# Four reciprocal square roots move from GpSimd to ScalarE, and three weight splits change place in a two-block transformer kernel

## The chip, the cores and the metric
The kernel runs on one core of one Trainium2 chip. The metric is the device time of one execution in microseconds (us), from the first to the last work of the program. Five engines work side by side and meet only at semaphores: TensorE (PE: matmuls and transposes), VectorE (DVE), ScalarE (ACT), GpSimd (POOL) and SyncE (SP), which here issues the loads from HBM.

## The reference
Two transformer blocks of two layers each run one after the other on 256 tokens of 1024 features, all in float32. Cut to what matters here:

```python
for i in range(2):                                   # first block
    xn = rmsnorm(h, norm_mix[i])
    h = h + hybrid_mixer(xn, w_in[i], ...)           # differential, forgetting and retention heads
    xn = rmsnorm(h, norm_ffn[i])
    h = h + (swiglu(...) if i == 0 else moe_swiglu(...))      # dense, then 8 experts, top 2
    gate = sigmoid(rmsnorm(h, ple_norm[i]) @ ple_gate[i])
    h = h + gate * (p[i] @ ple_proj[i])
# in hybrid_mixer, for the four differential heads of 128 columns:
    o_a = o[:, :, 0] - lam * o[:, :, 1]
    o_a = rmsnorm(o_a, subln_g) * (1 - lam_init)     # root 1: 8 roots a token row (2 tiles x 4 heads)

for l in range(2):                                   # second block
    proj = rms_norm(x, norm_g[l]) @ w_in[l]          # q_a, k_a, v_a, q_h, f_h, i_h, q_m, z
    kv_m = rms_norm(mem, mem_norm_g[l]) @ w_mem_kv[l]
    km = rms_norm(k_m, mem_k_norm[l])
    qm = rms_norm(q_m, mem_q_norm[l])                # root 2: again 8 a row
    y = concat([o_a, o_h, o_m]) * silu(z)
    x = x + y @ w_out[l]
```

## The kernel before, in words
Tokens lie in two tiles of 128 partitions. Every weight is streamed once from HBM in pieces of 1 MB (128 partitions x 2048 numbers). To get float32 accuracy from TensorE, ACT copies a piece to `high` in a rounded format (`split` in the ACT program, L1364), DVE subtracts it from the raw piece to get `low` (L1847), and PE does three matmuls for each product: high by high, high by low and low by high (`exact`, L700 to L702). So each piece goes SP load, ACT high, DVE low, then 24 (or 48 narrower) matmuls on PE. Activations are split in the same manner: PE turns rows, ACT writes the high half of the turned rows (L1380), DVE the low half (L1869).

There is no scheduler. Each engine has its program written out by hand, and the place of a split in it is set by calls: `splits(done)` makes all pieces up to three beyond `done` that have not been made, `split_next()` makes the next one. Only three `high`/`low` buffers exist, so ACT's `high` of a piece waits until PE has used the piece three before it (`pieces_used`). An engine works strictly in its own order; what stands behind an instruction that waits, waits too.

A reciprocal square root is asked for in two ways. `rstd_ask` writes mean square plus epsilon into `stat` on DVE, ACT answers with Sqrt (`serve_sqrt`, L1388), DVE takes the reciprocal (`rstd_answer`, L1900). ACT keeps one set of function tables; between Exp (the softmax, L1472) and Sqrt stands a table load. The second way, `root_ask`, hands the same `stat` to POOL, which raises it to the power -0.5 (L1835), and DVE goes on at `root_answer` without a reciprocal. It serves four places: in `attention1` of each layer (steps i == 9 and 10), for the differential heads, and in `attention2` (steps 2 and 3), for the memory queries `qm`. `attention1` and `attention2` are software pipelines over 12 heads: at step i, PE makes scores of head i, turns the weights of head i-1 and multiplies values for head i-2, and between these does the projections of later weights. In `attention1` the projections end with i == 9; at i == 10 ACT takes `v` and `sg` out of banks 6 and 7, PE then writes the turned retention queries and keys there (L875), and ACT goes on to Exp of head 10.

The expert layer is followed by a branch on an overflow flag (ACT L1718, DVE L2526, PE too). In its usual arm stands `embedding_in(1)`, which makes two splits with `split_next()`: one at its start and one at its end. Behind the branch follow `splits`, the memory rows' norm (`mem_sums`, `mem_norm`) and `embedding_out` on PE. Below, pg0 and pg1 are the two halves of the first gate weight of layer 1, pg2 the next piece, km0, km1, vm0, vm1 and qa0 the pieces of the memory keys, memory values and first queries of the second block, in the order of the stream.

## Time and profile before
| | |
|---|---|
| time, median of 3 runs | 2024.94 us (2024.91 to 2027.08) |
| the profiled execution's own time | 2024.91 us |
| its span, first to last instruction | 2023.1 us |
| PE, DVE, ACT, POOL busy | 97%, 76%, 61%, 0% |
| read from HBM | 501.73 MB, 249 GB/s over the span |

PE is busy for nearly the whole span, so what counts is time in which PE stands still. A timeline row reads: start, duration, engine, line, operation, and in brackets the idle time before it with what ended it. Matmuls overlap: the distance between starts, not the duration, is the pace (about 0.23 us for 512 columns at the full clock).

### The profile page before, as it was taken

The numbers are of one execution on the slowest core, as the hardware profiler recorded it, in microseconds if no ns is written. First come the engines' busy times: TensorE is split into PE (matmuls) and PEld (weight loads), VectorE is DVE, ScalarE is ACT, GpSimd is POOL, SyncE is SP. The second block draws the span as 40 slices with busy tenths as digits, with TensorE's granted clock in tenths as the row PEclk, the third lists the DMA queues.
The fourth block names the chain that finished last, engine by engine and source line by source line (L and its number), as shares of the span: only waits on it lengthen the run. The fifth ranks groups of instructions, "written<-read, shape, count | busy, mean of one in ns | idle before, by whom it ended". The sixth has DMA issues, their size and how long they took to land.

```text
span 2023.1 us, 27402 instructions
## 1 busy us (share of the span) xinstructions
PE 1960.2 (97%) x10513; PEld 1670.3 (83%) x10513; DVE 1541.1 (76%) x1509; ACT 1232.5 (61%) x1332; POOL 6.8 (0%) x8
## 2 busy tenths in 40 slices
PE   8999999999899999999999999999998998999998
PEld 7879998887788888888888888888887887888887
DVE  5565555656788988889888898888887855876576
ACT  4555445554677777777777777777777544354442
POOL 0000000000000000000000000000000000000000
PEclk9999999999999999999999999999999999999999
DMA  8607554522799999999999999999976541345311
GB/s 262 223 30 268 188 187 147 173 99 80 266 374 351 351 375 330 373 342 359 373 330 374 340 359 375 330 374 336 363 290 220 187 161 69 125 155 199 126 63 42
DMA packets 243316, 504.08 MB, mean 249 GB/s; under 512 B 12184, under 2 KB 59032, under 8 KB 243224
## 3 DMA queue, kind: packets, MB, share of 16 engines
q1 hardware_dynamic: 242936, 502.71, 69.7%
q8 instruction: 63, 1.03, 0.2%
q14 instruction: 29, 0.24, 0.0%
q10 hardware_dynamic: 288, 0.11, 0.0%
HBM read 501.73 MB, written 1.05 MB: 249 GB/s over the span
## 4 chain that ended last, share of the span: by engine, by line
PE 83%; DVE 10%; ACT 4%; issue 2%; DMA 0%; DVEq 0%; ACTq 0%
PE bank L700 25%; PE bank L702 25%; PE bank L701 25%; DVE low L1847 4%; ACT high L1364 2%; PE bank L1171 1%; PE bank L1119 1%; PE bank L671 1%; PE bank L824 1%; ACT high L1566 1%; PE bank L1271 1%; DVE negmax L2029 1%; PE bank L793 1%; PE bank L815 1%; DVE y_lo L2482 1%
## 5 line engine op out<-in xcount | busy, mean ns | idle before, releaser
L2433 DVE TENSOR_TENSOR low<-raw,high 128x2048 fp32r<-128x2048 f32 x336 | 768.4, 2291 | 103.8 <-ACT high L1566 102.4
L1566 ACT ACTIVATE high<-raw 128x2048 fp32r<-128x2048 f32 x336 | 644.8, 1920 | 245.5 <-PE bank L702 244.7
L1847 DVE TENSOR_TENSOR low<-raw,high 128x2048 fp32r<-128x2048 f32 (+1 forms) x138 | 310.4, 2260 | 177.8 <-ACT high L1364 177.4
L1364 ACT ACTIVATE high<-raw 128x2048 fp32r<-128x2048 f32 (+1 forms) x138 | 260.7, 1894 | 170.2 <-PE bank L702 155.0
L700 PE MATMUL bank<-high,xg_hi 128*128 128x512 f32 x896 | 353.6, 395 | 0.8 <-DVE xg_lo L2416 0.8
L702 PE MATMUL bank<-high,xg_lo 128*128 128x512 f32 x896 | 349.5, 390 | 0.0
L701 PE MATMUL bank<-low,xg_hi 128*128 128x512 f32 x896 | 348.8, 389 | 0.0
L700 PE MATMUL bank<-high,xT_hi 128*128 128x512 f32 (+1 forms) x576 | 226.8, 394 | 5.7 <-issue 2.1
L702 PE MATMUL bank<-high,xT_lo 128*128 128x512 f32 (+1 forms) x576 | 221.5, 385 | 0.0
L701 PE MATMUL bank<-low,xT_hi 128*128 128x512 f32 (+1 forms) x576 | 221.0, 384 | 0.0
L700 PE MATMUL bank<-high,hT_hi 128*128 128x512 f32 x536 | 210.1, 392 | 0.0
L701 PE MATMUL bank<-low,hT_hi 128*128 128x512 f32 x536 | 208.7, 389 | 0.0
L702 PE MATMUL bank<-high,hT_lo 128*128 128x512 f32 x536 | 208.7, 389 | 0.0
L700 PE MATMUL bank<-xT_hi,high 128*128 128x256 f32 x672 | 193.2, 288 | 5.4 <-ACT v L1512 2.3
L702 PEld LDWEIGHTS bank<-high,xg_lo 128*128 128x128 f32 x896 | 168.1, 188 | 35.8
L700 PEld LDWEIGHTS bank<-high,xg_hi 128*128 128x128 f32 x896 | 168.3, 188 | 34.9 <-issue 1.1
L701 PEld LDWEIGHTS bank<-low,xg_hi 128*128 128x128 f32 x896 | 168.4, 188 | 33.7
L701 PE MATMUL bank<-xT_lo,high 128*128 128x256 f32 x672 | 191.3, 285 | 0.0
L702 PE MATMUL bank<-xT_hi,low 128*128 128x256 f32 x672 | 191.3, 285 | 0.0
L700 PEld LDWEIGHTS bank<-xT_hi,high 128*128 128x128 f32 x672 | 130.3, 194 | 7.3 <-ACT v L1512 2.7
L700 PEld LDWEIGHTS bank<-high,xT_hi 128*128 128x128 f32 x576 | 108.3, 188 | 27.8 <-issue 3.0
L701 PEld LDWEIGHTS bank<-xT_lo,high 128*128 128x128 f32 x672 | 130.3, 194 | 0.3
(326 smaller groups left out, 2328.4 us busy)
## 6 DMA issues: line engine op xcount, KB each, us to landing
raw<-in_moe_w_gate SPq DMA_DIRECT2D x112, 1024.0 KB, 5.5
raw<-in_moe_w_up SPq DMA_DIRECT2D x112, 1024.0 KB, 5.5
raw<-in_moe_w_down SPq DMA_DIRECT2D x112, 1024.0 KB, 5.6
raw<-in_w_in SPq DMA_DIRECT2D x63, 1024.0 KB, 5.3
raw<-in_w_out SPq DMA_DIRECT2D x20, 1024.0 KB, 4.8
raw<-in_dense_w_gate SPq DMA_DIRECT2D x11, 1024.0 KB, 5.2
raw<-in_dense_w_up SPq DMA_DIRECT2D x11, 1024.0 KB, 5.4
raw<-in_dense_w_down SPq DMA_DIRECT2D x11, 1024.0 KB, 5.0
```

The lines of the kernel that those rows point to most:

```text
L671: last = pe.transpose(bank_of(key)[:, (k * NT + t) * P:(k * NT + t + 1) * P], rows[:, t, (2 * j + k) * P:(2 * j + k + 1) * P], ident[:, :])
L700: pe.matmul(dst, stationary[0], moving[0], start=start, stop=False)
L701: pe.matmul(dst, stationary[0], moving[1], start=False, stop=False)
L702: return pe.matmul(dst, stationary[1], moving[0], start=False, stop=stop)
L793: pe.matmul(bank[(g + i) % 2][:, c0:c0 + n], q[:, tok(t)], k[:, 0:n], start=(t == 0), stop=False)
L815: last = pe.transpose(bank[2 + g % 2][:, b * P:(b + 1) * P], probs[:, g % 2, b * P:(b + 1) * P], ident[:, :])
L824: last = pe.matmul(att_out(name, u, t), probsT[:, g % 2, c0 + s * P:c0 + (s + 1) * P], val[:, s, :], start=(s == 0), stop=(s == n // P - 1))
L1119: last = pe.transpose(b[:, f * P:(f + 1) * P], hm[:, j % 2, f * P:(f + 1) * P], ident[:, :])
L1364: act.activation(high[:, slot, 0:k * n], raw[:, raw_slot[piece], 0:k * n], ACT.Copy).then_inc(high_done, 1)
L1566: act.activation(high[:, k % PARTS, :], raw[:, slot, :], ACT.Copy).then_inc(s["high"], 1)
L1847: dve.tensor_tensor(low[:, slot, 0:k * n], src, high[:, slot, 0:k * n].bitcast(F32), ALU.subtract).then_inc(low_done, 1)
L2433: dve.tensor_tensor(low[:, k % PARTS, :], raw[:, at0 + k % slots, :], high[:, k % PARTS, :].bitcast(F32), ALU.subtract).then_inc(s["low"], 1)
```

## The change
The four roots of POOL go to ACT: its program, its two semaphores and the constant `minus_half` are gone, `rstd_ask` and `rstd_answer` stand in DVE's program instead, and ACT gets a `serve_sqrt` at i == 10 of `attention1` and at i == 2 of `attention2`. In `attention2` the ask and the answer now stand together at step 2 (`head_squares`); before, the answer was taken at step 3. The split at the end of `embedding_in(1)` is gone on ACT and DVE, so that the next `splits`, behind the branch, makes that piece. And DVE's `splits(km[0])` behind `norm_rows(("mix2", l))` is gone: for l == 0 it had nothing left to make, for l == 1 it made vm0 and vm1.

```diff
@@ ACT, attention1
                     if i == 10:
+                        sqrt_ahead()
+                        serve_sqrt(8)
                         act.wait_ge(rotated, l + 1)
@@ ACT, attention2
                         splits(pieces_of[("qh", "fh", "ih")[(i - 1) // 2], l][(i - 1) % 2])
+                    if i == 2:
+                        serve_sqrt(2 * 4)
@@ ACT, embedding_in
                 norm_high(("ple", l))
-                if not table:
-                    split_next()
@@
-        @block.gpsimd
-        def _(pool):
-            for n in range(2 * LAYERS):
-                pool.wait_ge(root_asks, n + 1)
-                pool.tensor_tensor(stat[:, 1, 0:8], stat[:, 0, 0:8], minus_half[:, :], ALU.pow).then_inc(root_answers, 1)
@@ DVE, attention1
-                        root_ask(ysum[:, :], 1.0 / P)
+                        rstd_ask(ysum[:, :], 8, 1.0 / P)
                     if i == 10:
-                        root_answer()
+                        rstd_answer(8)
@@ DVE, attention2
                     if i == 2:
-                        squares_of(qm, 4, P)
-                        root_ask(rinv[:, 0:8], 1.0 / P)
+                        head_squares(qm, 4, P)
                     if i == 3:
-                        root_answer()
                         gained(qm, 4, P, g_mem[:, 0, l, :]).then_inc(normed, 1)
@@ DVE, embedding_in
                 norm_low(("ple", l))
-                if l == 1:
-                    split_next()
@@ DVE, second block
                 norm_rows(("mix2", l))
-                splits(pieces_of["km", l][0])
                 for i in range(NT):
                     take(("km", l, i), km_rows[:, i * G:(i + 1) * G])
```

What ACT does in `attention1` around step 10, before (`sg` and `v` are the copies out of banks 6 and 7, `probs` the Exp of head 10):

```order
L1364 ACTIVATE high<-raw 128x2048 [waits pieces_used,slot4_landed]
L1518 ACTIVATE sg<-bank,rst 128x256 [waits pieces_used,rotated]
L1520 ACTIVATE v<-bank,rst 128x256
L1518 ACTIVATE sg<-bank,rst 128x256 [waits pieces_used]
L1520 ACTIVATE v<-bank,rst 128x256
L1472 ACTIVATE probs,rowsum<-bank,negmax 128x128 [waits att_turned,att_max]
L1472 ACTIVATE probs,rowsum<-bank,negmax 128x256
```

The same place after:

```order
L1362 ACTIVATE high<-raw 128x2048 [waits pieces_used,slot4_landed]
L1397 ACT_TABLE_LOAD
L1397 ACTIVATE marks<-ident 128x1
L1386 ACTIVATE stat<-stat 128x8 [waits dve_asks]
L1518 ACTIVATE sg<-bank,rst 128x256 [waits pieces_used,rotated]
L1520 ACTIVATE v<-bank,rst 128x256
L1518 ACTIVATE sg<-bank,rst 128x256 [waits pieces_used]
L1520 ACTIVATE v<-bank,rst 128x256
L1470 ACT_TABLE_LOAD [waits att_turned]
L1470 ACTIVATE probs,rowsum<-bank,negmax 128x128 [waits att_max]
```

Two table loads and two small activations have come in ahead of Exp, three of the four ahead of the copies.

What DVE does in layer 1 of the second block between the norm of the rows (`yf<-h,stat`) and the low half of the turned rows (`xT_lo`), before; the two `low` are vm0 and vm1, the single one is qa0:

```order
L1965 TENSOR_SCALAR yf<-h,stat 128x1024
L1847 TENSOR_TENSOR low<-raw,high 128x2048 [waits high_parts_done] x2
L1997 COPY km_rows<-bank 128x512 [waits pieces_used] x2
L1847 TENSOR_TENSOR low<-raw,high 128x2048 [waits high_parts_done]
L1869 SCALAR_TENSOR_TENSOR xT_lo<-bank,gcols,xT_hi 128x256 [waits high_rows_taken]
```

And after:

```order
L1948 TENSOR_SCALAR yf<-h,stat 128x1024
L1980 COPY km_rows<-bank 128x512 [waits pieces_used] x2
L1840 TENSOR_TENSOR low<-raw,high 128x2048 [waits high_parts_done] x3
L1862 SCALAR_TENSOR_TENSOR xT_lo<-bank,gcols,xT_hi 128x256 [waits high_rows_taken]
```

The copies, which wait until PE has used km1, now stand ahead of vm0 and vm1.

What ACT does around the end of the overflow arm, before (the program text has both arms in a row; the jump leads to the row behind it; slot2 holds pg1, slot3 pg2):

```order
L1380 ACTIVATE xT_hi<-bank,gcols 128x256
L1364 ACTIVATE high<-raw 128x2048 [waits pieces_used,slot2_landed]
L1724 UNCONDITIONAL_BRANCH
L1364 ACTIVATE high<-raw 128x2048 [waits pieces_used,slot3_landed]
L1448 ACTIVATE kT,mem_sum<-mem_rows 128x1024 [waits mem_in]
```

After:

```order
L1378 ACTIVATE xT_hi<-bank,gcols 128x256
L1724 UNCONDITIONAL_BRANCH
L1362 ACTIVATE high<-raw 128x2048 [waits pieces_used,slot2_landed]
L1362 ACTIVATE high<-raw 128x2048 [waits pieces_used,slot3_landed]
L1446 ACTIVATE kT,mem_sum<-mem_rows 128x1024 [waits mem_in]
```

The high half of pg1 has moved from ahead of the jump to behind it; DVE's low half has moved likewise. The orders of PE and SP are the same in both kernels.

## Rows read from the trace of the kernel before

**Rows 1.** The page's busy times: engine, us, share of the span, instructions.
```profile
PE 1960.2 (97%) x10513; PEld 1670.3 (83%) x10513; DVE 1541.1 (76%) x1509; ACT 1232.5 (61%) x1332; POOL 6.8 (0%) x8
```

**Rows 2.** Core span and mean granted clock; then the page's chain by engine.
```profile
core 0: 2023.1 us, clock 0.990
...
PE 83%; DVE 10%; ACT 4%; issue 2%; DMA 0%; DVEq 0%; ACTq 0%
```

**Rows 3.** Waits: waiter <- waited for: us in total, times, longest.
```profile
ACT high L1364 <- DMA raw<-in_w_in: 9.3, 4, 7.6
```

**Rows 4.** ACT's groups by line: table load for Exp, and Sqrt answers.
```profile
L1472 ACT ACT_TABLE_LOAD x6 | 7.7, 1283 | 0.1
...
L1388 ACT ACTIVATE stat<-stat 128x2 f32<-128x2 f32 (+3 forms) x21 | 4.4, 208 | 31.0 <-DVE stat L1895 24.0 <-DVE stat L1952 4.5 <-DVE stat L2224 1.6
```

**Rows 5.** Timeline of ACT, attention1 of layer 0 around step 10.
```profile
111.57 0.48 ACT L1520 ACTIVATE v<-bank,rst 128x256 f32<-128x256 f32 x1
113.49 0.37 ACT L1472 ACTIVATE probs<-bank,negmax 128x128 f32<-128x128 f32 x1 [1.44 <-DVE negmax L2029]
```

**Rows 6.** Timeline of PE, the same stretch.
```profile
114.46 0.90 PE L815 MATMUL bank<-ident,probs 128*128 128x128 f32 x3 [1.70 <-ACT probs L1472]
...
117.61 1.23 PE L936 MATMUL bank<-qT,kT 64*128 64x256 f32 x4 [1.07 <-ACT kT L1461]
```

**Rows 7.** Timeline of ACT, the same place in layer 1.
```profile
471.99 0.37 ACT L1472 ACTIVATE probs<-bank,negmax 128x128 f32<-128x128 f32 x1 [1.44 <-DVE negmax L2029]
```

**Rows 8.** Timeline of DVE, then ACT and PE, attention2 of layer 0.
```profile
1647.71 0.17 DVE L1912 TENSOR_SCALAR stat<-rinv 128x8 f32<-128x8 f32 x1
...
1651.53 0.69 DVE L1997 COPY at<-bank 128x512 f32<-128x512 f32 x1 [0.78 <-PE bank L702]
...
1652.79 0.37 ACT L1472 ACTIVATE probs<-bank,negmax 128x128 f32<-128x128 f32 x1 [4.36 <-DVE negmax L2029]
...
1659.27 0.50 PE L815 MATMUL bank<-ident,probs 128*128 128x128 f32 x3
```

**Rows 9.** Timeline of DVE, layer 1 of the second block.
```profile
1794.89 4.49 DVE L1847 TENSOR_TENSOR low<-raw,high 128x2048 fp32r<-128x2048 f32 x2 [0.19 <-ACT high L1364]
1800.07 1.29 DVE L1997 COPY km_rows<-bank 128x512 f32<-128x512 f32 x2 [0.69 <-PE bank L702]
1802.08 2.29 DVE L1847 TENSOR_TENSOR low<-raw,high 128x2048 fp32r<-128x2048 f32 x1 [0.72 <-ACT high L1364]
```

**Rows 10.** Timeline of PE there: the first matmul of vm0.
```profile
1799.87 0.39 PE L700 MATMUL bank<-high,xm_hi 128*128 128x512 f32 x1
```

**Rows 11.** Timeline of ACT, then DVE, then PE, around the jump behind the experts.
```profile
1529.05 1.98 ACT L1364 ACTIVATE high<-raw 128x2048 fp32r<-128x2048 f32 x1
1537.00 1.92 ACT L1364 ACTIVATE high<-raw 128x2048 fp32r<-128x2048 f32 x1 [5.97 <-issue]
...
1541.79 1.42 DVE L1979 TENSOR_SCALAR mem_rows<-mem_rows,stat 128x1024 f32<-128x1024 f32 x2
...
1535.93 0.47 PE L700 MATMUL bank<-high,xT_hi 128*128 128x512 f32 x1 [2.12 <-issue]
...
1543.26 1.97 PE L671 MATMUL bank<-ident,mem_rows 128*128 128x128 f32 x16 [1.61 <-DVE mem_rows L1979]
```

**Rows 12.** Stretches: engine busy (instructions), then granted clock (PEclk), DMA share, GB/s.
```profile
114.10:120.90 6.80, 5.37 (x26) 4.79 (x26) 2.04 (x5) 5.20 (x13) 0.00 (x0) 0.50 0.01 2
...
1861.70:1865.20 3.50, 3.50 (x22) 2.85 (x19) 3.50 (x6) 1.29 (x4) 0.00 (x0) 0.51 0.56 156
```

**Rows 13.** Timeline of PE: the same kind of matmul at the lower and the full clock.
```profile
1863.83 0.41 PE L700 MATMUL bank<-xT_hi,high 128*128 128x256 f32 x1
1864.04 0.41 PE L701 MATMUL bank<-xT_lo,high 128*128 128x256 f32 x1
...
1865.49 0.28 PE L700 MATMUL bank<-xT_hi,high 128*128 128x256 f32 x1
1865.61 0.28 PE L701 MATMUL bank<-xT_lo,high 128*128 128x256 f32 x1
```

More of the change, by code:

```diff
@@ L185, in program @@
         stat = sb("stat", [P, 2, 16])
-        minus_half = sb("minus_half", [P, 8])
         ssum = sb("ssum", [P, 2, NT])
@@ L249, in program @@
         dve_asks, act_answers = sem("dve_asks"), sem("act_answers")
-        root_asks, root_answers = sem("root_asks"), sem("root_answers")
         setup_dve, squares = sem("setup_dve"), sem("squares_summed")
@@ L1905, in rstd @@
                 rstd_answer(n)
-            roots = [0]
-            def root_ask(sums, scale):
-                roots[0] += 1
-                dve.tensor_scalar(stat[:, 0, 0:8], sums, scale, EPS, ALU.mult, ALU.add).then_inc(root_asks, 1)
-            def root_answer():
-                dve.wait_ge(root_answers, roots[0])
             def rms(name):
@@ L2673, in _ @@
             dve.wait_ge(first_in, FIRST)
-            dve.memset(minus_half[:, :], -0.5)
             link(dve.memset(lone[:, :], 0.0))
```

## The prediction
> **What bounds the kernel now.** I read the page's busy times and its chain first. PE is busy for 97% of the span and is 83% of the chain; POOL works for 6.8 us in all [rows 1, 2]. So POOL's four roots can hardly be what the kernel waits for, and an edit shows only where it makes PE stand still or shortens a standstill. Then the waits: only one line waits long for a load, 9.3 us in four pieces, at the start of the program [rows 3]. Behind that, all waits are for another engine. So there is no load that keeps its own time and takes up a delay: what is lost at one place is still lost at the end. Last, the timelines of the six places the edits touch: attention1 twice, attention2 twice, the jump behind the experts, and the start of layer 1 of the second block.
>
> **Part 1, attention1 (both layers): +3.0 us.** ACT gets, ahead of Exp of head 10, a table load for Sqrt, two small activations and a load back for Exp. A load takes 1283 ns and ACT stands idle at most 0.1 us in all before six of them; a small activation takes about 208 ns [rows 4]. Together 2 x 1.28 + 2 x 0.2 = 2.97 us. Before, ACT ends its copies at 111.57 + 0.48 = 112.05 and stands idle for 1.44 us until DVE has the maxima of head 10 [rows 5]. So Exp starts 2.97 - 1.44 = 1.5 us later. Does PE feel it? Its idle time of 1.70 us ahead of turning the weights ends by exactly this Exp, and its next, 1.07 us, by ACT's copy of the turned keys, which ACT reaches without a pause from that Exp on [rows 6]. So PE is late by the same 1.5 us. In layer 1 the row is the same [rows 7]: twice 1.5 = 3.0 us. DVE's added reciprocal, two tenths, lies behind maxima that ACT is by then too late to use. Bounds: if the small activations overlap to a tenth each, 1.3 us a layer; if the loads use nothing of the idle time, 2.97 us. I take 1.5, the sum of the nearest rows.
> The Trainium skill, "ScalarE: Activation LUTs", section "What ACT_TABLE_LOAD costs", gives 1283 ns for the load and about 1380 ns of draining more, 2.66 us for every switch of sets. By it this part would be 2 x 2.66 + 0.4 - 1.44 = 4.3 us a layer. The trace agrees on the load and not on the drain: the idle time before six loads is 0.1 us together [rows 4].
>
> **Part 2, attention2 (both layers): 0.** DVE asks at 1647.71 + 0.17 = 1647.88. ACT, free at 1652.79 - 4.36 = 1648.4, loads (1.28), takes the root (0.2), and DVE can go on at 1650.0 with a reciprocal and then its next low half, some 1.7 us later than before. Half of that is covered, since DVE stood waiting for PE ahead of its copy at 1651.53 anyway; about 0.9 us remains, and Exp of head 3, at 1652.79 before, comes at 1653.7. ACT's load back fits: it stood idle 4.36 us there. PE wants these weights only at 1659.27, behind the projection of the second forget piece [rows 8]. That projection is the cover; without it the cost would be 0.9 us a layer. Bounds 0 and 1.8, I take 0.
>
> **Part 3, vm0 and vm1 behind the copies: +3.75 us.** Before, DVE makes both low halves at 1794.89, while PE still works on km, and PE goes on with vm0 at 1799.87 without a pause [rows 9, 10]. Now the copies come first, and they wait for the last matmul of km1, as they did: 1800.07. They take 1.29 us, less a tenth of overlap, so vm0's low half runs from 1801.27 to 1803.56 [rows 9], and PE starts vm0 at about 1803.6. 1803.6 - 1799.87 = 3.75 us during which PE has nothing else. vm1 and qa0 follow at 2.2 us each, and a piece is some 5.7 us of PE's work (pg1's, from 1535.93 to 1543.26 less 1.61 [rows 11]), so they are in time, and nothing behind is waiting for a load. Bounds of this term: 3.5 to 3.8.
>
> **Part 4, the clock behind that standstill: +1.5 us.** PE's granted clock is the full 2.4 GHz nearly everywhere (mean 0.990 [rows 2]), but 1.2 GHz in a few stretches, each begun at a standstill: 3.5 us at 1861.7, and 6.8 us at 114.1 about the pause of 1.70 us [rows 12]. At the lower level matmuls of 256 columns start 0.21 us apart (1863.83, 1864.04), at the full one 0.12 (1865.49, 1865.61) [rows 13]: nearly half the time of such a stretch is lost. The new pause of 3.75 us is longer than each of those. If a stretch like the shorter one follows, 3.5 x 0.43 = 1.5 us; like the longer one, 2.9; none, 0. I take 1.5, by the stretch in the same layer with matmuls at work.
>
> **Part 5, pg1 behind the jump: +1.0 us.** Before, ACT makes the high half of pg1 at 1529.05, then stands idle for 5.97 us though nothing that the profile shows holds it, and goes on at 1537.00; PE stands 2.12 us at the same jump and starts pg1 at 1535.93 [rows 11]. Now pg1's high and low (1.9 and 2.3 us) follow the jump. Three readings. (a) ACT's pause is as short as PE's: it goes on at 1529.1 + 2.1 = 1531.2, pg1 is ready at 1535.4, PE loses nothing, the memory's norm comes early, and PE's later pause of 1.61 us [rows 11] goes: -1.6. (b) The pause stays 5.97 us but starts when the high half would have: ACT goes on at 1535.0, pg1 is ready at 1539.3, PE ends it at 1545.0 where it was to be free for the memory rows at 1543.26: +1.7. (c) ACT met the jump while its last work still ran, and goes on at 1537.0 as before: pg1 ready 1541.2, PE done 1546.9, +3.6. Between -1.6 and +3.6 I take the middle, 1.0, since PE's row and ACT's pull to either side.
> The Trainium skill, "Runtime: NRT & Kernel Launch", section "Instruction fetch mechanics", says that a taken branch to code that is not held stops the engine until that code is fetched; the trace agrees that engines stand at this jump, by 2.12 and 5.97 us. By that rule work moved behind the jump loses its cover, which is reading (b) or (c): the sum would be 0.7 to 2.6 us higher.
>
> Removed at the start is one DVE memset ahead of work that waits for ACT: 0. POOL's end does not matter.
>
> **Sum.** 3.0 + 0 + 3.75 + 1.5 + 1.0 = 9.25 us. The profiled execution took 2024.91 us (span 2023.1), practically the median of 2024.94. 2024.9 + 9.25 = 2034.2 us, 0.46% slower.
>
> **Rivals.**
> *Pauses without a price in clock, and a jump that costs nothing.* 3.0 + 3.75 = 6.75, so 2031.7 us. For it: mid-size pauses such as 2.12 and 1.61 us [rows 11] appear with a mean clock of 0.990. Against it: none of the pauses in these rows is as long as 3.75 us.
> *The jump in full.* Reading (c) and a long low stretch: 3.0 + 3.75 + 2.9 + 3.6 = 13.25, so 2038.2 us. For it: the fetch rule and the 5.97 us. Against: it takes both at once.
> *Each switch drains.* By rows the mechanism would be that ACT cannot start a load until its queue is empty and starts late behind it; at 1.4 us more for each of four loads in attention1 it gives 9.25 + 5.6, 2039.8 us. Against: 0.1 us of idle time before six loads.
> *Not slower: the clock pays it back.* A mean of 0.990 with two levels means 2 x 0.010 x 2023 = 40 us at 1.2 GHz, worth at most 20 us if PE were dense in all of them. Later or shifted pauses could leave some of these stretches at the full clock. It decides from 9 us, that is if half of all low time went and that time was dense; the stretch at 114.10 is not (5.37 us busy of 6.8, most of it waiting on ACT [rows 12]). It would end at about 2024 us. Little speaks for it, since this change adds pauses.
>
> **Chances.** The forecast with its near neighbours (2032.5 to 2036.5) 0.50; first rival (to 2032.5) 0.27; the jump in full 0.10; draining 0.03; not slower 0.05; parts 1 or 3 smaller than read, 2027 to 2030, 0.05. Range 2030.0 to 2038.2 us. A difference of under 0.2% (4 us) can't be told from none here. Slower by more, above 2029.0: 0.93; within: 0.05; faster: 0.02.
>
> **What would show it.** Part 1: PE idle 3.2 us instead of 1.70 ahead of turning the weights of head 10 in both layers, two table loads between, and PE's score matmul of retention at 119.1. Part 2: Exp of head 3 one microsecond later, PE's row unmoved. Part 3: a wait of PE for DVE's low of 3.7 us at vm0, the only new one in that layer. Part 4: granted clock at one half right behind it. Part 5: how late PE starts pg1, against 1535.93 and the shift up to there, and whether the pause before the memory rows is still there. I am wrong if vm0 starts without a pause, if ACT's two loads vanish in its idle time, or if later pauses shrink by what was lost.

## The result and the profile after

The changed kernel took 2039.51 us (median of 4 runs, 2039.0 to 2044.16) against 2026.01 us of the kernel before beside it: ratio 1.0063, 95% interval 1.0051 to 1.0076. I had forecast 2034.2 us, at most 2038.2. The direction was right and the amount too small: 13.5 us between the medians, or 12.8 by the ratio, for 9.25. The profiled execution took 2038.04 us, with a span of 2036.3 us, 13.2 us more than before.

The core's line, then the page's busy times and its chain by engine:

```profile
core 0: 2036.3 us, clock 0.986
```
```profile
PE 1967.3 (97%) x10513; PEld 1675.3 (82%) x10513; DVE 1540.8 (76%) x1512; ACT 1243.3 (61%) x1346; POOL 0.2 (0%) x4
...
PE 83%; DVE 9%; ACT 5%; issue 2%; DMA 0%; DVEq 0%; ACTq 0%
```

Against [rows 1, 2]: the same 10513 matmuls keep PE busy 7.1 us longer, and the mean clock has gone from 0.990 to 0.986. A clock of 0.986 over this span is 2 x 0.014 x 2036 = 57 us at 1.2 GHz, 17 us more than the 40 of the kernel before, and matmuls last longer there [rows 13]. That is the first sign of where the forecast missed.

To see where the time went I laid PE's instructions of both traces side by side and read at which of them the start falls further behind. It moves by more than 0.2 us only here (each figure is the step from one level stretch of the delay to the next):

| place | standstill: forecast | measured | clock: forecast | measured |
|---|---|---|---|---|
| attention1, layer 0 | 1.5 | 1.6 | 0 | 3.9 |
| attention1, layer 1 | 1.5 | 1.6 | 0 | 0 |
| attention2, both | 0 | 0 | 0 | 0 |
| jump and pg1 | 1.0 | 1.4, and 1.8 given back at the memory rows | 0 | 1.5 |
| 1632 and 1686 us | - | 0 | 0 | 1.5 - 1.2 |
| vm0 | 3.75 | 3.8 | 1.5 | 2.5 |
| 1862 us | - | 0 | 0 | -1.4 |
| sum | 7.75 | 6.6 | 1.5 | 6.8 |

13.4 us, less 0.3 us by which the program began earlier, is the 13.2 us of the span within a tenth.

**Attention1.** The timeline of ACT in layer 0, then of PE (start, busy time, engine, line, instruction; in brackets the idle time ahead of it and who ended it):

```profile
110.30 1.28 ACT L1397 ACT_TABLE_LOAD   x1
111.59 0.20 ACT L1397 ACTIVATE marks<-ident 128x1 f32<-128x1 f32 x1
111.70 0.19 ACT L1386 ACTIVATE stat<-stat 128x8 f32<-128x8 f32 x1
...
113.36 1.28 ACT L1470 ACT_TABLE_LOAD   x1
114.66 0.37 ACT L1470 ACTIVATE probs<-bank,negmax 128x128 f32<-128x128 f32 x1
```
```profile
112.76 1.43 PE L873 MATMUL bank<-ident,a 128*128 128x128 f32 x8 [1.69 <-ACT v L1520]
115.62 0.90 PE L813 MATMUL bank<-ident,probs 128*128 128x128 f32 x3 [1.43 <-ACT probs L1470]
...
118.77 0.81 PE L934 MATMUL bank<-qT,kT 64*128 64x256 f32 x2 [1.08 <-ACT kT L1459]
```

Against [rows 5, 6] Exp of head 10 comes 1.17 us later and the score matmul of retention 1.16, and 0.3 us more against the program's earlier start. ACT's 1.44 us of idle time are gone, as forecast, but the lateness shows up one step earlier than I said: ACT does its first load ahead of the copies of v, so PE first stands 1.69 us behind `v` and then again 1.43 behind Exp, two pauses of middle size (3.1 us together) where there was one of 1.70. The rest is in the clock. The stretches of the changed kernel at these places (window, its length, PE's busy time, granted clock, DMA share, GB/s):

```profile
113.80:130.90 17.10, 14.59 (x64) 0.50 0.00 1
479.00:485.80 6.80, 5.14 (x24) 0.50 0.00 0
1544.00:1547.40 3.40, 3.24 (x8) 0.50 0.59 169
1639.50:1643.00 3.50, 3.50 (x19) 0.51 0.81 260
1810.20:1817.00 6.80, 5.21 (x12) 0.50 0.61 211
1861.70:1877.00 15.30, 13.10 (x70) 1.00 0.40 137
```

In layer 0 PE has 1.2 GHz for 17.1 us, where it had it for 6.8 [rows 12]. The longer stretch reaches over dense projections behind the pauses, and there it costs. The last row shows the opposite: the stretch that [rows 12] have at 1861.70 is gone. Before, it follows a pause of 2.21 us at the start of attention2 in layer 1. The changed kernel has that pause too, at full clock, and instead a stretch of 3.4 us behind the same pause in layer 0 (the row at 1639.50). So the same pause at the same instruction brings low clock in one trace and none in another.

**Jump.** Timelines of ACT, DVE and PE:

```profile
1539.84 3.71 ACT L1362 ACTIVATE high<-raw 128x2048 fp32r<-128x2048 f32 x2 [3.77 <-issue]
...
1541.81 4.49 DVE L1840 TENSOR_TENSOR low<-raw,high 128x2048 fp32r<-128x2048 f32 x2 [4.67 <-ACT high L1362]
...
1546.86 1.42 DVE L1962 TENSOR_SCALAR mem_rows<-mem_rows,stat 128x1024 f32<-128x1024 f32 x2
...
1544.16 0.80 PE L698 MATMUL bank<-high,xT_hi 128*128 128x512 f32 x1 [3.51 <-DVE low L1840]
...
1551.22 1.03 PE L669 MATMUL bank<-ident,mem_rows 128*128 128x128 f32 x8
```

PE stands idle 3.51 us ahead of pg1 instead of 2.12, and its 1.61 us ahead of the memory rows [rows 11] are no more. ACT's pause is 3.77 us instead of 5.97.

**vm0.** Timelines of DVE and PE:

```profile
1808.16 1.29 DVE L1980 COPY km_rows<-bank 128x512 f32<-128x512 f32 x2 [5.38 <-PE bank L700]
1809.37 6.68 DVE L1840 TENSOR_TENSOR low<-raw,high 128x2048 fp32r<-128x2048 f32 x3
...
1811.80 0.77 PE L698 MATMUL bank<-high,xm_hi 128*128 128x512 f32 x1 [3.67 <-DVE low L1840]
1812.36 0.63 PE L699 MATMUL bank<-low,xm_hi 128*128 128x512 f32 x1
1812.79 0.63 PE L700 MATMUL bank<-high,xm_lo 128*128 128x512 f32 x1
```

The standstill is the one forecast. Around it the clock is at half for 6.8 us, and the matmuls of 512 columns behind it are 0.43 to 0.56 us apart.

**Attention2.** Timeline of ACT, then DVE:

```profile
1657.80 1.28 ACT L1386 ACT_TABLE_LOAD   x1
1659.09 0.21 ACT L1386 ACTIVATE stat<-stat 128x8 f32<-128x8 f32 x1
1659.32 1.28 ACT L1470 ACT_TABLE_LOAD   x1
1663.03 0.37 ACT L1470 ACTIVATE probs<-bank,negmax 128x128 f32<-128x128 f32 x1 [2.42 <-DVE negmax L2012]
...
1659.33 0.20 DVE L1893 RECIPROCAL stat<-stat 128x8 f32<-128x8 f32 x1 [2.09 <-ACT stat L1386]
```

DVE waits 2.09 us for the root and ACT still has 2.42 us to spare ahead of Exp; PE does not notice.

### The profile page after: what moved, and what is told of

It is laid out like the page before. It is cut to its first block, busy times and chain, and to the rows that moved or that the text cites. A ratio compares the mean times of both kernels' runs of the same rounds, so it can differ in the third digit from the quotient of the medians.

```text
span 2036.3 us, 27415 instructions
## 1 busy us (share of the span) xinstructions
PE 1967.3 (97%) x10513; PEld 1675.3 (82%) x10513; DVE 1540.8 (76%) x1512; ACT 1243.3 (61%) x1346; POOL 0.2 (0%) x4
## 4 chain that ended last, share of the span: by engine, by line
PE 83%; DVE 9%; ACT 5%; issue 2%; DMA 0%; DVEq 0%; ACTq 0%
PE bank L698 25%; PE bank L700 25%; PE bank L699 25%; DVE low L1840 3%; ACT high L1362 2%; PE bank L1169 1%; PE bank L1117 1%; PE bank L669 1%; PE bank L822 1%; ACT high L1568 1%; PE bank L1269 1%; DVE negmax L2012 1%; DVE y_lo L2463 1%; PE bank L791 1%; PE bank L813 1%
```

## The experiments

Each kernel ran on one chip together with the kernel before; ratios are to that. The kernel before varies by itself: of 116 executions of it beside these experiments, 29 show a mean clock of 0.986 or 0.987 and took 2032.8 to 2037.8 us, and the 66 fastest-clocked (0.990 to 0.992) took 2021.5 to 2028.9 us. So one trace is one draw, and a difference of 3 us in the medians can stay undecided. "Overwritten matmuls" are matmuls into a bank that the next real work writes anew; the outputs don't depend on them. All of them come from one helper:

```diff
+            def busy(dst, x, n):
+                for _ in range(n):
+                    pe.matmul(dst[:, :], x[:, 0, 0:P], x[:, 0:2, :].rearrange("p a b -> p (a b)"), start=True, stop=True)
```

### Each part alone

**Roots of attention1 alone**, on the kernel before:

```diff
@@ ACT, attention1
                     if i == 10:
+                        sqrt_ahead()
+                        serve_sqrt(8)
                         act.wait_ge(rotated, l + 1)
@@ POOL: two roots are left
-            for n in range(2 * LAYERS):
+            for n in range(LAYERS):
@@ DVE, attention1, steps 9 and 10
-                        root_ask(ysum[:, :], 1.0 / P)
+                        rstd_ask(ysum[:, :], 8, 1.0 / P)
-                        root_answer()
+                        rstd_answer(8)
```

> The kernel before with the two roots of attention1 alone on ACT (the two of attention2 stay on POOL, the splits where they were). The clock theory: PE's own delay is 1.6 us in each layer, 3.2 in all, and whatever more there is comes with TensorE at 1.2 GHz for longer than before in one of the two places, up to 3.4 us: 2028 to 2032 us against 2024.9. The rival, that each of the two loads drains ACT: 4.3 us a layer whatever the clock, and 8.6 in all at the full clock.

Measured: 2032.21 us, ratio 1.0030 [1.0019, 1.0041]. PE's three pauses are those of the changed kernel (timeline of PE), and the stretch behind them is as long:

```profile
111.46 1.75 PE L875 MATMUL bank<-ident,a 128*128 128x128 f32 x8 [1.71 <-ACT v L1522]
114.32 0.90 PE L815 MATMUL bank<-ident,probs 128*128 128x128 f32 x3 [1.11 <-ACT probs L1472]
```
```profile
108.00:133.00 25.00, 21.10 (x111) 0.66 0.00 1
470.00:495.00 25.00, 20.65 (x117) 0.73 0.00 1
```

A clock of 0.66 over 25 us is 17.1 us at half speed, 0.73 is 13.6 us. So this part alone costs 6 us by the ratio, twice the 3.0 forecast for its standstills and just above the 2028 to 2032 us that I had expected. In the trace PE's rows lose 1.5 us by the standstill and 3.8 by the clock in layer 0, 1.5 and 3.0 in layer 1. The span is 8.1 us longer, near the 8.6 us of the draining rival, but by another way: ACT's loads stand with no idle time around them here too.

One thing more is in this trace. ACT's pause at the jump, which this edit doesn't touch, has fallen from 5.97 us:

```profile
1541.83 1.91 ACT L1364 ACTIVATE high<-raw 128x2048 fp32r<-128x2048 f32 x1 [2.11 <-issue]
```

**Roots of attention2 alone:**

```diff
@@ ACT, attention2
+                    if i == 2:
+                        serve_sqrt(2 * 4)
@@ POOL: two roots are left
-            for n in range(2 * LAYERS):
+            for n in range(LAYERS):
@@ DVE, attention2, steps 2 and 3
-                        squares_of(qm, 4, P)
-                        root_ask(rinv[:, 0:8], 1.0 / P)
+                        head_squares(qm, 4, P)
-                        root_answer()
```

> The kernel before with the two roots of attention2 alone on ACT. Both the clock theory and the forecast: PE's rows there don't move, DVE waits about 2.1 us for the root and Exp of head 3 is some 1 us late, the time within 1 us of before. The rival, that the blocked DVE reaches PE: 1 to 2 us a layer, PE waiting for DVE or ACT in the projections of fh or ih.

Measured: 2026.86 us, ratio 1.0007 [0.9991, 1.0022], and in the trace PE has no idle time behind the root's step that it didn't have before. DVE waits 2.09 us for the root, as expected. Part 2 holds.

**km copies ahead of vm's first piece, alone:**

```diff
@@ DVE, second block
                 norm_rows(("mix2", l))
-                splits(pieces_of["km", l][0])
```

> The kernel before without the splits ahead of the copies of the memory keys, alone. The clock theory: PE waits 3.7 us for vm0's low half and is 3.9 us late, and then works at 1.2 GHz for 3 to 7 us, which costs 1.4 to 2.4 more, of which later places may give back up to 1.3: 4 to 6.5 us over before. The rival, that only the wait counts and the rest of the loss came from elsewhere: 3.9 us.

Measured: 2032.91 us, ratio 1.0033 [1.0019, 1.0048]: 6.7 us by the ratio, the upper end of the clock theory, where the wait alone would give 3.9. In the trace PE loses 3.8 us at the standstill and 5.4 us by the end of the low clock behind it (1802.8 to 1806.2 us); the span grew by 3.7 us only, since PE had been 0.8 us ahead and won 0.9 us further on. The timeline of PE:

```profile
1802.87 0.77 PE L700 MATMUL bank<-high,xm_hi 128*128 128x512 f32 x1 [3.67 <-DVE low L1847]
```

**pg1 behind the jump, alone:**

```diff
@@ ACT, embedding_in
                 norm_high(("ple", l))
-                if not table:
-                    split_next()
@@ DVE, embedding_in
                 norm_low(("ple", l))
-                if l == 1:
-                    split_next()
```

> The kernel before with the split of pg1 behind the jump, alone. The clock theory: PE starts pg1 1.5 us late, works at 1.2 GHz for a while (1.3 us), and gets 1.5 us back ahead of the memory rows: +0 to +1.5 us. The code theory (ACT stands at the jump until the code behind it has come, and once more at the end of a piece of code, which lies at another row when rows ahead of it change): ACT's pause is about 3.8 us before its first high half as in the changed kernel or a little more, and a second pause of up to 4 us can stand between the two high halves or behind them, since this kernel has six ACT instructions fewer ahead of the jump's target than the changed one; then the memory norm is late and up to 3 us are lost there.

Measured: 2028.15 us, ratio 0.9998 [0.9982, 1.0014]. The trace shows why this is so little: 3.64 us of idle time instead of 2.12, a stretch of 6.8 us at half clock behind it, and the pause ahead of the memory rows gone. Timelines of ACT and PE:

```profile
1533.81 3.71 ACT L1364 ACTIVATE high<-raw 128x2048 fp32r<-128x2048 f32 x2 [3.94 <-issue]
...
1538.10 0.80 PE L700 MATMUL bank<-high,xT_hi 128*128 128x512 f32 x1 [3.64 <-DVE low L1845]
...
1546.59 1.91 PE L671 MATMUL bank<-ident,mem_rows 128*128 128x128 f32 x16
```

In its trace PE ends 3.3 us later, 2.7 of them at the jump; in its times nothing is to be seen. What remains of this part is between 0 and 3 us; the runs can't say more.

### The pauses filled

**The changed kernel, all three pauses of attention1 filled** (7 ahead of the mixed rows, 6 ahead of the turn, 4 ahead of the keys):

```diff
+                    if i == 11:
+                        pe.wait_ge(att_copied, first + 9)
+                        busy(bank[2 + (first + 10) % 2], xT_hi, 6)
...
                     if i == 10:
+                        busy(bank[2 + (first + 10) % 2], xT_hi, 7)
                         pe.wait_ge(rotated, l + 1)
...
                     if i == 11:
+                        busy(bank[2 + (first + 11) % 2], xT_hi, 4)
                         emptied(pe, ("kcT", l))
```

> The changed kernel with 7, 6 and 4 matmuls whose results are overwritten, put on PE into its three pauses of attention 1 (ahead of the wait for the mixed rows, ahead of the turn of the head after it, ahead of the wait for the keys), in both layers; the outputs stay the same. Clock theory: the engine's pauses bring the low-clock stretch (17.1 us in layer 0 of the changed kernel, against 6.8 before), so with the pauses filled the stretch goes or falls to 6.8 us or less; 3.4 us come back in layer 0, the standstill of 1.6 us itself stays; with the stretches that the kernel before has too gone as well, up to 2 us more. 2035 us (2033 to 2037), ratio to the kernel before 1.0045. Rival (the 3.4 us are a wait for something else, or the clock falls with the clock's own rhythm whatever PE does): the stretch stays at 17 us, 2039.5 us, ratio 1.0065 or a little more by the matmuls added.

Measured: 2031.44 us, ratio 1.0017 [1.0002, 1.0031]. No low clock is left in attention1 of either layer (in attention2 of layer 0 it still is, 6.8 us from 1682.3 us), and 8 us came back by the medians, more than the 4.5 I expected. The windows:

```profile
108.00:133.00 25.00, 23.89 (x153) 1.00 0.00 1
470.00:495.00 25.00, 23.88 (x144) 1.00 0.06 16
```

Side by side with the changed kernel, PE is 5.6 us earlier behind the stretch of layer 0 and 1.4 us in layer 1. From 37 to 115.9 us its rows lie 0.3 us earlier, and at 118.77 us, where retention's score matmul waits for ACT, it is 0.3 us again. The edit adds work and takes none away, and what PE waits for ends when it did; so it is the clock that gave this back. Not all of it is the change's price: the same filling gives the kernel before 1.6 and 1.5 us at these places (below). The change's own share is 5.6 - 1.6 = 4.0 us in layer 0 and nothing in layer 1, in these traces.

**The changed kernel, 14 matmuls ahead of vm0 in layer 1:**

```diff
+                if l == 1:
+                    free_bank(pe, vm[0])
+                    busy(bank_of(vm[0]), xm_hi, 14)
                 rows_half(vm, ("vm", l), 0, rows=(xm_hi, xm_lo))
```

> The changed kernel with 14 matmuls of 512 columns whose result is overwritten, put on PE ahead of the first product of the expert vm in layer 1, where it stands still for 3.67 us behind the km copies; the outputs stay the same. Clock theory: the low clock at 1810.2 to 1817.0 us goes, PE's rows behind vm0 come 2.3 us earlier than in the changed kernel, while the standstill of 3.9 us stays. What the change had gained further on (a stretch at 1862 us that the changed kernel lacks, 1.3 us) may come back as a loss. 2037.5 us (2036 to 2039), ratio 1.0055. Rival (the 2.3 us are DVE's late copies for the pieces behind vm0, not the clock): PE's rows keep their 6.2 us of delay, 2039.5 us, ratio 1.0065.

Measured: 2037.91 us, ratio 1.0048 [1.0034, 1.0062], within what the clock theory gives, though the intervals overlap. Timeline of PE and window:

```profile
1811.32 3.33 PE L711 MATMUL bank<-xm_hi 128*128 128x512 f32 x14
1815.15 0.47 PE L698 MATMUL bank<-high,xm_hi 128*128 128x512 f32 x1 [0.50 <-DVE low L1848]
```
```profile
1795.00:1825.00 30.00, 29.50 (x138) 1.00 0.58 208
```

vm0 starts as late as in the changed kernel, but at full clock: 2.4 us later on are back in PE's rows. This is the price of the clock behind the vm0 standstill in the changed kernel's trace. (vm0 holds memory values; no expert is involved.)

**The same filling on the kernel with only the km copies moved:**

> The kernel before with the km copies ahead of vm's first piece, as in the changed kernel (and nothing else of the change), and 14 overwritten matmuls on PE ahead of vm0 in layer 1; the outputs stay the same. Clock theory: against the same edit without the matmuls (2032.9 us) the low clock behind vm0 goes (1.5 to 2.3 us) and the standstill of 3.75 us stays: 2030.5 us (2029 to 2032), ratio 1.002. Rival (what PE loses behind vm0 is DVE's late copies): 2033 us, ratio 1.0033.

Measured: 2033.56 us, ratio 1.0019 [1.0001, 1.0038], against 1.0033 without the matmuls: inconclusive by the times, and in microseconds what the rival gave. The trace shows the low clock at vm0 gone, PE 4.0 us late there instead of 5.4, and something I had not asked for: in attention1, which this kernel doesn't touch, PE had 1.2 GHz for 13.6 us (0.73 over 108 to 133 us) and was 3.9 us late. So the long stretch can also come without the roots.

**Which of the pauses holds the clock down?** The new one alone filled (only the 7 of the first filled kernel):

> The changed kernel with 7 overwritten matmuls on PE in the one pause of attention 1 that the change adds (1.69 us ahead of the mixed rows), in both layers; the two pauses behind it stay as they are, and the outputs stay the same. Theory (the added standstill is what lengthens the stretch at 1.2 GHz): the stretch is 6.8 us or less again, as in the kernel before, and 3.4 us in layer 0 come back: 2036 us (2034.5 to 2037.5), ratio 1.0045. Rival (the two old pauses, now behind a late start, hold the clock down): the stretch starts later but stays over 10 us, 2039 us, ratio 1.006.

The two old ones filled (6 and 4), the new one left empty:

> The changed kernel with 6 and 4 overwritten matmuls on PE in the two pauses of attention 1 that the kernel before has too; the added standstill of 1.69 us stays empty, and the outputs stay the same. Theory (the added standstill alone brings the length): a stretch of 1.2 GHz over 7 us stays behind 112 us and 2037 to 2039 us are measured, ratio 1.006. Rival (pauses add up, whichever they are): the stretch goes or falls to 7 us, and the time is 2032 to 2035 us, ratio 1.003 to 1.0045, near the kernel with all three filled.

Measured: 2040.59 us, ratio 1.0056 [1.0034, 1.0077] with the new one filled, and 2031.63 us, ratio 1.0010 [0.9994, 1.0026] with the old ones filled. First the windows of the former, then of the latter, then PE's timeline of the latter:

```profile
108.00:133.00 25.00, 21.52 (x135) 0.93 0.00 1
470.00:495.00 25.00, 21.52 (x110) 0.73 0.00 1
```
```profile
108.00:133.00 25.00, 22.20 (x149) 1.00 0.11 38
470.00:495.00 25.00, 22.19 (x149) 1.00 0.00 1
```
```profile
116.94 1.30 PE L881 MATMUL bank<-ident,a 128*128 128x128 f32 x8 [1.70 <-ACT v L1529]
```

My theory that the added standstill alone brings the long stretch falls. With it in place and the other two filled, the clock doesn't drop in attention1; with it filled and the others open, the stretch was 3.4 us in one layer and 13.6 in the other, and the median stayed at that of the changed kernel (2040.43 us on the same chip, below). All 12 executions with the old ones filled had a mean clock of 0.990 to 0.993, all 8 with the new one filled 0.986 to 0.988, so this is no accident of two traces. The pauses have to stand together; what sets the length of the stretch they bring stays open.

The trace with the old ones filled shows something else. Its standstill ahead of vm0 is unfilled and 3.67 us long as ever, and no low clock follows:

```profile
1795.00:1825.00 30.00, 26.33 (x124) 1.00 0.48 172
```

PE is 2.4 us better off there than in the changed kernel. The same pause of 3.67 us brought 6.8 us at 1.2 GHz in four traces, 3.4 in two and none in this one, so its price in clock was 0 to 2.5 us.

**Both kernels profiled anew:**

> The kernel before, unchanged, profiled anew. If a program's stretches at 1.2 GHz are fixed: 6.8 us at 114 and at 472 us again, ratio 1.000. If they vary from one execution to the next: other lengths at the same places, ratio 1.000 all the same.

> The changed kernel, unchanged, profiled anew. If a program's stretches are fixed: 17.1 us at 113.8 and 6.8 us at 479 us again, and ratio 1.0063. If they vary freely: a stretch under 10 us at 114 us, as often in the kernel before; ratio 1.005 to 1.007 all the same.

Measured: 2026.11 us, ratio 0.9992 [0.9971, 1.0013], and 2040.43 us, ratio 1.0058 [1.0040, 1.0077]. The windows of the kernel before, then of the changed one:

```profile
108.00:133.00 25.00, 21.71 (x137) 0.86 0.00 1
470.00:495.00 25.00, 22.10 (x130) 0.86 0.00 1
```
```profile
108.00:133.00 25.00, 21.06 (x108) 0.66 0.00 1
470.00:495.00 25.00, 20.62 (x113) 0.73 0.00 1
```

0.86 is 6.8 us again. The changed kernel has 17.1 us again in layer 0, and 13.6 us in layer 1, where its first profile had 6.8: 2.9 us more at that place. Over all kernels that fill none of attention1's pauses, layer 0 shows 17.1 us in 5 of 5 traces with the roots, and 6.8 us in 5, 3.4 in one and 13.6 in one of those without them; layer 1 shows 6.8 or 13.6 with the roots, never more than 6.8 without. The roots don't create the stretch; they make a long one the rule.

**The changed kernel with the pauses of attention1, attention2 and vm0 filled** (7, 7, 4; 9, 8, 7, in both layers; the 14 ahead of vm0, in layer 1 alone, where its pause is):

> The changed kernel with overwritten matmuls of 512 columns on PE in the pauses of both attentions (7, 7 and 4 in attention 1; 9, 8 and 7 in attention 2) and 14 ahead of vm0, in both layers; the outputs stay the same. Clock theory (the change costs its own standstills and, apart from them, low clock that these pauses bring): hardly a stretch at 1.2 GHz is left, and what stands between it and the kernel before with its pauses filled (2020.2 us) is the sum of the standstills, 3.3 (attention 1) + 0 (attention 2) + 3.9 (vm0) + up to 1.0 (the jump) = 7 to 8 us: 2028 us (2026.5 to 2029.5), ratio to the kernel before 1.001. Rival (the change's other 6 us are waits of ACT and DVE that the filling of PE doesn't touch): 2033 us or more, ratio 1.0035.

Measured: 2028.74 us, ratio 1.0006 [0.9994, 1.0019]. The filling gives 11 us back in one and the same kernel. Beside the kernel before with its pauses filled (below) it is 8.6 us slower by the medians (on two chips), 9.9 by the ratios and 10.7 by the spans. That is more than the 7 to 8 I had counted. PE's rows of these two fall apart by 1.5 us in each attention1 and 4.0 at vm0, which are the standstills; then by 2.3 at the jump (a stretch of low clock from 1536.8 us, 6.8 us long, is still there) and 1.5 behind a later stretch, with 0.4 given back at the router. So the clock's price goes where the pauses are filled, but part of it turns up at pauses left open: of the 13.2 us that the change costs in span, filling both kernels takes away only 2.5.

### The kernel before, improved

**Its pauses filled** (7 and 4 in attention1; 9, 8 and 7 in attention2):

```diff
+                busy(bank[6], xT_hi, 9)
                 emptied(pe, ("qm", l, 1))
```

> The kernel before with overwritten matmuls in PE's pauses of both attentions (7 and 4 in attention 1; 9, 8 and 7 in attention 2), in both layers; the outputs stay the same. Clock theory: the stretches at 1.2 GHz at 114.1, 472.5, 520.3 and 1680.8 us (6.8 us each) go, each worth 1 to 1.5 us where PE has the path: 2021 us (2019 to 2024), ratio 0.998. Rival (clock stretches are moved to another place rather than removed, or the matmuls push real work back): 2025.5 to 2028, ratio 1.000 to 1.001.

Measured: 2020.18 us, ratio 0.9957 [0.9941, 0.9972]: faster than both kernels. PE's rows gain 1.6, 1.5, 1.3, 1.5 and 1.2 us at five of the six stretches; that at the router is left, begins 5.8 us earlier and costs 1.2 us more.

**Four activations at ACT's start:**

```diff
+            for k in range(4):
+                act.activation(spare[:, k:k + 1], marks[:, 60:61], ACT.Sqrt)
```

> The kernel before with four activations of one column on ACT at the start, into columns that nothing reads, so that ACT's code behind the jump out of the expert loop lies four instructions further on; the outputs stay the same. Theory (ACT's 5.97 us of issue at the jump are two fetches of code in a row, the second at a border of the code that now lies just behind the jump): the pause changes to about 3.8 us, as where the high half stands behind the jump, and PE's pause of 1.61 us ahead of the memory rows falls: 2024.3 us (2023 to 2026), ratio 0.9992. Rival (the pause comes with the jump alone, wherever the code lies): it stays at 6.0 us and PE's at 1.6, 2025.8 us, ratio 1.000.

Measured: 2026.76 us, ratio 0.9991 [0.9974, 1.0007]: the times can't tell. In the trace ACT's pause at the jump falls from 5.97 to 2.12 us (my theory had given 3.8) and PE's 1.61 us ahead of the memory rows go. Timeline of ACT:

```profile
1534.14 1.91 ACT L1365 ACTIVATE high<-raw 128x2048 fp32r<-128x2048 f32 x1 [2.12 <-issue]
```

The trace with the roots of attention1 alone, whose added activations also lie ahead of the jump, has 2.11. With pg1's high half ahead of the jump the pause was 5.97 to 6.11 us in the six traces that add nothing to ACT's program up to there, and 2.04 to 2.12 in the three that do. So its length hangs on where in ACT's program the jump stands, and not on the jump alone. That it is code being fetched is my reading; no view shows the fetch.

**The same four on the changed kernel:**

> The changed kernel with the four activations of one column on ACT at the start; the outputs stay the same. Code theory: ACT's pause at the jump, 3.77 us, holds two fetches of its code; with the code four instructions further on it falls to about 2.1 us, as in the kernel before with the same four, and PE's idle time ahead of pg1 falls from 3.51 to about 2.1 us, which its own jump sets: 2038 us (2037 to 2039), ratio 1.0055, and with the low clock behind that pause gone 2037. Rival (the pause of 3.77 us comes with the jump wherever the code lies, or 2.1 is only had with the high half ahead of the jump): 2039.5 us, ratio 1.0065, PE's idle time ahead of pg1 3.5 us.

Measured: 2039.66 us, ratio 1.0061 [1.0039, 1.0083]; ACT's pause 3.67 us, PE's idle time ahead of pg1 3.66. The rival holds. With pg1's high half behind the jump the pause was 3.67 to 3.95 us in all nine traces, wherever the code lay. Why 2.1 isn't reached there stays open.

**Filling, the four activations, and 9 matmuls ahead of the router's ranks:**

> The kernel before with PE's pauses in both attentions filled, 9 more overwritten matmuls ahead of the ranks of the router, and four activations of one column on ACT at the start, which shift its code behind the jump; the outputs stay the same. Clock theory with the code theory: the stretch at 514.5 us goes too (about 1 us), and PE's pause ahead of the memory rows (1.8 us): 2017.5 us (2016 to 2019.5), ratio 0.9945. Rival (the two gains don't add up, since at the jump another resource takes over or the clock falls elsewhere): 2020 us, ratio 0.9957.

Measured: 2017.10 us, ratio 0.9942 [0.9922, 0.9963], the lowest median of all, though its interval overlaps that of the filling alone (0.9957). The core's line and the timeline of PE:

```profile
core 0: 2016.0 us, clock 0.998
```
```profile
524.78 0.47 PE L701 MATMUL bank<-high,xg_hi 128*128 128x512 f32 x1 [3.48 <-DVE xg_lo L2434]
```

The gain at the jump is there (2.1 us in PE's rows, with a pause of ACT of 2.04 us). That of the router is not: the low stretch moved from 514.5 to 525.2 us, into dense work behind a pause of 3.48 us at the first expert, and PE's rows lose 0.6 us there. Another 1.6 us go to a stretch at 1907.6 us that the filling alone doesn't have, so the span is only 0.5 us shorter (2016.0 for 2016.5), and that the time met the forecast of 2017.5 is partly luck.

## Why the prediction was wrong

**What bounds the kernel** held: every delay of PE that didn't come back through the clock or the jump stayed to the end.

**Part 1** was right in its size (1.6 us in each layer for 1.5) and wrong in one detail: PE meets the delay first behind the copies of v, so that there are three pauses in a row and not two. I looked at which instruction ends the wait and left out that the first load stands ahead of other work on ACT that PE needs too.

**Part 2** held, 0.

**Part 3** held: 3.8 us for 3.75.

**Part 4 is the step that failed.** "If a stretch like the shorter one follows, 3.5 x 0.43 = 1.5 us" priced the clock at one place and put it at nothing everywhere else. Measured: 2.5 us at vm0 (6.8 us long), 3.9 in attention1 of layer 0 and 1.5 at the jump, with some losses and gains further on: 6.8 us for 1.5. The largest piece is attention1's. Taken off, it would leave 2035.6 us, inside the range. I had the rows for it in hand. [Rows 12] show a stretch that begins at attention1's pause of 1.70 us, so pauses of that size are enough, and I was about to lengthen exactly that place. Filling PE's pauses there shows it: with the standstills of real work left as they are, 5.6 us come back in layer 0, and only 1.6 when the kernel before is filled in the same way. The 17.1 us stretch stood there in five of five traces with the roots and in none of seven without them.

**Part 5**: 1.1 us for 1.0, and that is luck. I had added up standstills; these gave 1.4 - 1.8 = -0.4 us, and the clock, which I had left out here, 1.5. Of my three readings none was exact; (b)'s order was right, but ACT's pause was 3.77 us and not 5.97. The experiment with this edit alone leaves 0 to 3 us for it.

**The rivals.** The one without a price in clock is refuted by the filled kernels. "The jump in full" and "each switch drains" end near the measured time and are both wrong in their reason. The former's sum, 13.25 us, is even that of the spans, 13.2, by chance: at the jump 1.1 us were lost, not 3.6. And behind each load ACT goes on within 0.02 us (110.30 + 1.28 = 111.58, next at 111.59), so a forecast of 2039.8 by draining would have been right by chance too. "The clock pays it back" did happen in part (1.4 us at 1862, 1.2 at 1686), and far too little.

**The range** ended at 2038.2 because I let the clock vary at vm0 alone. With 0 to 3.9 us at each of the four places that get a pause its upper end would have been 2024.9 + 7.75 + 15.6 = 2048 us.

## What to carry to other kernels

When a change gives PE a pause, price two things: the pause, and the low clock behind it. The second is a range and starts at 0. For its upper end look in several traces for pauses of like size and read how long the clock stays at 1.2 GHz and how dense the work in it is. A pause put next to others can cost more than its own length, as here in layer 0 (1.6 us of pause, 4 us of clock). Where such pauses can't be removed, matmuls whose result is overwritten, as many as the pause holds, gave 0.43% on the kernel before and 11 us on the changed one.

## What the runs showed of the hardware

- The length of a stretch at 1.2 GHz behind the same cluster of pauses was 3.4, 6.8, 13.6 or 17.1 us in different traces, the same program's too (6.8 and 13.6 in layer 1 of the changed kernel). At one and the same place 17.1 us cost 5.6 us of PE's time and 6.8 us cost 1.6: the first part lies mostly over waiting, the rest over dense work.
- A single pause of 3.67 us was followed by 6.8 us at 1.2 GHz, by 3.4 or by none, and one of 2.21 us by 3.4 or none, at the same instructions in different traces. Executions of the unchanged kernel before differ by about 8 us between those with a mean clock of 0.987 (median 2033.4 us) and those with 0.990 or 0.991 (2025.4 and 2025.0).
- Filling two of three neighbouring pauses took the whole stretch away (one kernel, both layers); filling the third alone did not.
- A pause of ACT at a jump was 6.0, 3.8 or 2.1 us, depending on the order of the work and on a few small instructions over 1000 us earlier.
- Two table loads around small activations cost ACT what they last, 1.28 us each, and nothing more.
